# First block of a fused transformer kernel on one core: attention and retention heads in pairs between half tiles of the projections, a first tile by chunks of the input, first loads in row halves

## What is computed

```python
mod = jax.nn.silu(c) @ w_ada[l] + b_ada[l]              # six vectors of 1024: shift, scale, gate, twice
h = rmsnorm(x, g_pre_mix[l]) * (1.0 + scale_m) + shift_m
proj = h @ w_in[l]                                      # 1024 x 3072
rq, rk, rv, rg, aq, ak, av = jnp.split(proj, split_at, axis=-1)
y_ret = bidirectional_retention(...)                    # 4 heads, keys of 64, values of 128, then a norm per head
y_ret = jax.nn.silu(rg) * y_ret
results = [dilated_attention(qh, kh, vh, w, d, slopes) for (w, d) in DILATED_CONFIGS]   # 8 heads of 64
mixed = jnp.concatenate([y_ret, y_att], axis=-1) @ w_out[l]
x = x + gate_m * rmsnorm(mixed, g_post_mix[l])
```

## Time and profile before

| | us |
|---|---|
| median of 3 runs | 2343.58 (2340.36 to 2344.03) |
| the profiled execution, its own time | 2334.57 |
| its span in the trace | 2332.8 |
| TensorE busy in the span | 2016.2 (86%) |
| VectorE, ScalarE busy | 1017.2, 732.0 |
| DMA, mean over the span | 282 GB/s |

### The profile page before, as it was taken

One profiled execution on the slowest core, in us unless ns is written; L12 is line 12 of the kernel. 1 busy time (PEld: TensorE's weight loads), 2 busy tenths in 40 slices (PEclk: granted clock), 3 DMA queues, 4 the chain that ended last, 5 costly groups with the idle time before them and its releaser, 6 DMA issues.

```text
span 2332.8 us, 30652 instructions
## 1 busy us (share of the span) xinstructions
PE 2016.2 (86%) x12663; PEld 1489.7 (64%) x12664; DVE 1017.2 (44%) x1126; ACT 732.0 (31%) x794; POOL 31.7 (1%) x27
## 2 busy tenths in 40 slices
PE   7988867767777677776789999999999999999999
PEld 5858423323232233332278899998888889998887
DVE  5462100000000000000178677777777768777776
ACT  3452101000000000000144446454444444745443
POOL 0000000000000000000000002000000000200000
PEclk8997787888878888877799999999999999999999
DMA  9755699999999999999945565365575566545554
GB/s 327 285 203 242 248 428 428 429 428 428 430 428 428 429 428 428 429 428 428 419 169 179 152 225 181 132 217 181 152 221 187 158 184 208 181 152 192 181 156 133
DMA packets 235194, 657.03 MB, mean 282 GB/s; under 512 B 6932, under 2 KB 121940, under 8 KB 210516
## 3 DMA queue, kind: packets, MB, share of 16 engines
q1 hardware_dynamic: 235092, 655.62, 73.7%
HBM read 654.54 MB, written 1.05 MB: 281 GB/s over the span
## 4 chain that ended last, share of the span: by engine, by line
issue 85%; PE 13%; DVE 1%; POOL 1%; ACT 0%; DVEq 0%; POOLq 0%; ACTq 0%
PE psum L1101 3%; PE psum L1102 2%; PE psum L1123 2%; PE psum L1124 2%; PE psum L1125 2%; PE psum L1202 2%; PE psum L1203 1%; DVE ring_r L1935 1%; PE psum L1169 0%; POOL work L715 0%; ACT ring_r L1466 0%; PE psum L1170 0%; POOL work L714 0%; POOL work L716 0%; DVE x L2231 0%
## 5 line engine op out<-in xcount | busy, mean ns | idle before, releaser
L1935 DVE TENSOR_TENSOR ring_r<-ring,ring_r 128x2048 fp32r<-128x2048 f32 (+2 forms) x182 | 452.6, 2517 | 100.9 <-ACT ring_r L1466 100.1
L1101 PE MATMUL psum<-work_r,ring_r 128*128 128x512 f32 x1280 | 448.6, 396 | 3.5 <-DVE ring_r L1935 3.5
L1466 ACT CAST ring_r<-ring 128x2048 fp32r<-128x2048 f32 (+2 forms) x180 | 360.0, 2040 | 289.0 <-PE psum L1203 120.0
L1102 PE MATMUL psum<-work_r,ring_r 128*128 128x256 f32 x1280 | 358.0, 280 | 0.0
L1101 PEld LDWEIGHTS psum<-work_r,ring_r 128*128 128x128 f32 x1280 | 240.1, 188 | 61.2 <-issue 4.0
L1123 PE MATMUL psum<-work_r,ring_r 128*128 128x256 f32 x928 | 263.5, 284 | 2.5 <-DVE ring_r L1935 2.5
L1124 PE MATMUL psum<-work_r,ring_r 128*128 128x256 f32 x928 | 262.3, 283 | 0.0
L1125 PE MATMUL psum<-work_r,ring_r 128*128 128x256 f32 x928 | 262.0, 282 | 0.0
L1018 PE MATMUL psum<-ring,work 128*32 128x512 f32 x1536 | 216.0, 718 | 42.8 <-DMA ring<-in_w_up_e_dram 41.0
L1202 PE MATMUL psum<-work_r,ring_r 128*128 128x512 f32 x704 | 246.0, 395 | 3.0 <-DVE ring_r L1935 3.0
L1102 PEld LDWEIGHTS psum<-work_r,ring_r 128*128 128x128 f32 x1280 | 241.4, 189 | 0.0
(11 more groups left out here) (295 smaller groups left out, 2439.1 us busy)
## 6 DMA issues: line engine op xcount, KB each, us to landing
ring<-in_w_gate_e_dram SPq DMA_DIRECT2D x64, 2048.0 KB, 12.4
ring<-in_w_down_e_dram SPq DMA_DIRECT2D x48, 2048.0 KB, 31.7
ring<-in_ffn_w_up_dram SPq DMA_DIRECT2D x41, 2048.0 KB, 8.0
ring<-in_w_up_e_dram SPq DMA_DIRECT2D x32, 2048.0 KB, 21.4
work<-in_w_up_e_dram SPq DMA_DIRECT2D x32, 2048.0 KB, 30.1
ring<-in_w_in_dram SPq DMA_DIRECT2D x26, 2048.0 KB, 8.1
ring<-in_ffn_w_down_dram SPq DMA_DIRECT2D x32, 1408.0 KB, 7.1
work<-in_w_down_e_dram SPq DMA_DIRECT2D x16, 2048.0 KB, 37.6
```

What stands on the lines that cost most here:

```text
L1101: pe.matmul(dst, w_hi[:, k, cols], h_both(k), start=(k == 0), stop=False)
L1102: mm = pe.matmul(dst[:, 0:S], w_lo[:, k, cols], h_hi_[:, S * k:S * (k + 1)], start=False, stop=(k == KD - 1))
L1466: act.copy(hi_unit(name, unit), raw_unit(name, unit)).then_inc(hi_ready, 1)
L1935: dve.tensor_tensor(lo_unit(name, unit), raw_unit(name, unit), hi_unit(name, unit).bitcast(F32), ALU.subtract).then_inc(lo_ready, 1)
```

## The change

It rewrites the order of the first block and some of its buffers. (1) The tiles `ada` 0 to 3 are loaded as two pairs, each in two DMAs of four row chunks with 1024 columns in one piece; TensorE takes the four modulations as halves (`half_modulation`) with small matmuls between (`warm`). (2) The attention's tiles come first (`WIN`), the first of them in two DMAs, split chunk by chunk and multiplied chunk by chunk over all four column blocks (`head_tile`). The small loads now go ahead of the second `win` tile. (3) The other tiles are done in half tiles (`win_unit`), with an eviction for each half (`evict`), and the heads stand between them, two heads at a time: scores with the two heads on the upper and the lower 64 rows of the array, without zeroed halves, values on its left and right 64 columns. (4) The retention's values are centred by VectorE when they leave PSUM (`values_centred`), which replaces the mean matmul on the result. (5) `wout` is multiplied in four parts by chunks of the input, those of the attention first, with the retention's norm between them. (6) Slots 6 and 7 are released after the last head, and `EXPERT_SLOTS` begins with them.

The core of the diff (the new order of TensorE in full, of ScalarE and VectorE in parts):

```diff
+WIN = (3, 4, 5, 0, 1, 2)
...
-    order = [("ada", 0), ("ada", 1), ("ada", 2), ("ada", 3), ("win", 0), ("win", 1), ("ada", 4), ("win", 2), ("ada", 5),
-             ("win", 3), ("ada", 6), ("win", 4), ("ada", 7), ("win", 5), ("ada", 8), ("wout", 0), ("wout", 1),
-             ("ada", 9), ("ada", 10), ("ada", 11)]
-EXPERT_SLOTS = (2, 1, 3, 0, 4, 5, 6, 7, 8)
+    order = [("ada", 0), ("ada", 1), ("ada", 2), ("ada", 3), ("win", 3), ("win", 4), ("ada", 4), ("ada", 5), ("win", 5),
+             ("ada", 6), ("win", 0), ("ada", 7), ("win", 1), ("ada", 8), ("win", 2), ("ada", 9), ("wout", 0),
+             ("ada", 10), ("wout", 1), ("ada", 11)]
+EXPERT_SLOTS = (6, 7, 2, 3, 0, 1, 4, 5, 8)
...
+            def pair_half(i, half):
+                first = slot_view(("ada", i), KD, 512)
+                pair = ring[:, i:i + 2, :].rearrange("p s n -> p (s n)").rearrange("p (k n) -> p k n", k=KD)
+                src = a["w_ada"][0].rearrange("(k p) n -> p k n", p=P)
+                ks = slice(4 * half, 4 * half + 4)
+                sp.dma_start(pair[:, ks, :], src[:, ks, 512 * i:512 * i + 1024]).then_inc(loaded[i + half], 16)
+            for i in (0, 2):
+                for half in range(2):
+                    pair_half(i, half)
+            for name, _, _, _ in first_tiles()[4:]:
...
+                if name == ("win", 3):
+                    sp.wait_ge(tile_done[0], 1)
+                    view, src = slot_view(name, KD, 512), columns(w, 512 * i, 512)
+                    sp.dma_start(view[:, 0:4], src[:, 0:4]).then_inc(head_loaded, 16)
+                    sp.dma_start(view[:, 4:8], src[:, 4:8]).then_inc(loaded[0], 16)
...
+            def half_modulation(i, half):
+                pair = ring[:, i // 2 * 2:i // 2 * 2 + 2, :].rearrange("p s n -> p (s n)").rearrange("p (k n) -> p k n", k=KD)
+                w = pair[:, :, 512 * (i % 2):512 * (i % 2) + 512]
+                for k in range(4 * half, 4 * half + 4):
+                    g = k % 4
+                    mm = pe.matmul(mod_bank(i)[32 * g:32 * g + 32, :], silu_c[:, k, :], w[:, k, :],
+                                   start=(half == 0), stop=(half == 1), skip_group_check=True)
+                return mm
...
+            def warm(n):
+                for _ in range(n):
+                    pe.matmul(bank[5][:, 0:P], ident[:], ident[:], start=True, stop=True)
...
+            for i in (0, 2):
+                if i:
+                    pe.wait_ge(mod_ready, 2)
+                pe.wait_ge(loaded[i], 16)
+                half_modulation(i, 0)
+                half_modulation(i + 1, 0).then_inc(tile_done[i], 1)
+                if i:
+                    pe.wait_ge(scaled_ready, 1)
+                    warm(5)
+                pe.wait_ge(loaded[i + 1], 16)
+                half_modulation(i + 1, 1).then_inc(rows_done, 1)
+                half_modulation(i, 1).then_inc(tile_done[i + 1], 1)
+                modulation_columns(i + 1)
                 modulation_columns(i)
...
+            def head_tile():
+                pe.wait_ge(x_ready, 4)
+                name = ("win", 3)
+                for k in range(KD):
+                    h_chunk(k)
+                    pe.wait_ge(head_lo, k + 1)
+                    tokens = slice(S * k, S * (k + 1))
+                    for c in range(4):
+                        w_hi, w_lo = hi_unit(name, c // 2), lo_unit(name, c // 2)
+                        out_c, cols = two_banks[0][:, S * c:S * (c + 1)], slice(P * (c % 2), P * (c % 2 + 1))
+                        pe.matmul(out_c, w_hi[:, k, cols], h_hi_[:, tokens], start=(k == 0 and c % 2 == 0), stop=False,
+                                  skip_group_check=True)
+                        pe.matmul(out_c, w_hi[:, k, cols], h_lo_[:, tokens], start=False, stop=False, skip_group_check=True)
+                        mm = pe.matmul(out_c, w_lo[:, k, cols], h_hi_[:, tokens], start=False, stop=(k == KD - 1),
...
+            def win_unit(n):
+                i, half = WIN[n // 2], n % 2
                 name = ("win", i)
-                if i == 1:
-                    pe.wait_ge(x_ready, 4)
-                if i >= 2:
-                    pe.wait_ge(proj_ready, i - 1)
-                dst = two_banks[i % 2]
...
+            def att_scores(c):
+                if c == 0:
+                    pe.wait_ge(unit_evicted, 4)
+                    pe.wait_ge(ident_r_ready, 1)
+                else:
+                    pe.wait_ge(att_max_ready, 2 * c)
                 for t in range(TT):
-                    mm = pe.matmul(score_bank(hd)[:, S * t:S * (t + 1)], aq[hd % 2][:, c, P * t:P * (t + 1)],
-                                   ak[:, c, :], start=True, stop=True)
+                    for j in range(2):
+                        mm = pe.matmul(bank[4 + j][:, S * t:S * (t + 1)], aq[HALF * j:HALF * (j + 1), c, P * t:P * (t + 1)],
+                                       ak[HALF * j:HALF * (j + 1), c, :], start=True, stop=True)
...
+            def att_values(c):
+                if c == 0:
+                    pe.wait_ge(unit_evicted, 6)
+                pe.wait_ge(att_pT_ready, 2 * c + 2)
                 for s in range(TT):
-                    mm = pe.matmul(two_banks[1][at:at + ATT_DIM, S * c:S * (c + 1)],
-                                   av[:, s, ATT_DIM * hd:ATT_DIM * (hd + 1)], pT_att[:, s, :],
-                                   start=(s == 0), stop=(s == TT - 1), skip_group_check=True)
+                    for j in range(2):
+                        hd = 2 * c + j
+                        mm = pe.matmul(two_banks[1][HALF * j:HALF * (j + 1), S * c:S * (c + 1)],
+                                       av[:, s, ATT_DIM * hd:ATT_DIM * (hd + 1)], pT_att[:, j, s, :],
+                                       start=(s == 0), stop=(s == TT - 1), skip_group_check=True)
                 mm.then_inc(att_done, 1)
...
+            head_tile()
+            modulation(4)
+            layer_columns()
+            win_unit(2)
+            modulation_columns(4)
+            win_unit(3)
+            modulation(5)
+            att_scores(0)
+            win_unit(4)
+            modulation_columns(5)
+            win_unit(5)
+            att_transpose(0)
+            att_scores(1)
+            win_unit(6)
+            modulation(6)
+            att_transpose(1)
+            win_unit(7)
+            att_values(0)
+            att_transpose(2)
+            att_scores(2)
+            modulation_columns(6)
+            win_unit(8)
+            modulation(7)
+            att_transpose(3)
+            win_unit(9)
+            att_values(1)
+            att_transpose(4)
+            att_scores(3)
+            modulation_columns(7)
+            win_unit(10)
+            modulation(8)
+            att_transpose(5)
+            ret_scores(0)
+            win_unit(11)
+            att_values(2)
+            att_transpose(6)
+            modulation_columns(8)
+            ret_values(0)
+            ret_values(1)
+            ret_scores(1)
+            modulation(9)
+            att_transpose(7)
+            modulation_columns(9)
+            ret_values(2)
+            ret_values(3)
+            att_values(3)
+            modulation(10)
+            pe.wait_ge(att_done, ATT_HEADS // 2)
+            pe.wait_ge(ret_done, RET_HEADS)
+            for s in (6, 7):
+                pe.sem_inc(tile_done[s], 1)
+            def group_variances():
...
+            def wout_products(i, blocks, ks, opens=False, closes=False):
+                name = ("wout", i)
+                for c in blocks:
+                    unit, cols = c // 2, slice(P * (c % 2), P * (c % 2 + 1))
+                    pe.wait_ge(first_lo_ready, first_splits.ready(name, unit, 0))
+                    w_hi, w_lo = hi_unit(name, unit), lo_unit(name, unit)
+                    out_c = wout_banks(i)[:, S * c:S * (c + 1)]
+                    for k in ks:
+                        tokens = slice(S * k, S * (k + 1))
+                        pe.matmul(out_c, w_hi[:, k, cols], mixin_hi[:, tokens],
...
+            pe.wait_ge(mixin_lo_ready, 1)
+            wout_products(0, (0, 1), (4, 5), opens=True)
+            group_variances()
+            modulation_columns(10)
+            pe.wait_ge(mixin_lo_ready, 2)
+            wout_products(0, (0, 1), (6, 7))
+            spread_columns(grstd_ready, 1, two_banks[2], RET_HEADS * TT, grstd_spread)
+            wout_products(0, (2, 3), (4, 5, 6, 7), opens=True)
+            pe.wait_ge(centred_ready, 2)
+            wout_products(1, (0, 1), (4, 5, 6, 7), opens=True)
+            modulation(11)
+            wout_products(1, (2, 3), (4, 5, 6, 7), opens=True)
+            modulation_columns(11)
+            pe.wait_ge(mixin_lo_ready, 4)
             for i in range(2):
-                split_products(("wout", i), two_banks[i], mixin_hi, mixin_lo, mixin_chunk if i == 0 else None)
-            for s in range(SPLIT_SLOTS, SLOTS):
+                wout_products(i, (0, 1, 2, 3), (0, 1, 2, 3), closes=True)
+            for s in (4, 5, 8):
...
```

(26 more changed lines are left out.)

587 lines of the change are left out of this document (311 added, 276 removed).

## The result

| | before | after |
|---|---|---|
| median, 19 runs each (us) | 2339.91 (2332.74 to 2351.85) | 2325.22 (2317.03 to 2341.3) |
| the profiled execution, its own time | 2334.57 | 2326.23 |
| its span in the trace | 2332.8 | 2324.4 |

The ratio is 0.9941, with a 95% interval from 0.9924 to 0.9957: 13.8 us less (10.1 to 17.8). 14.5 were forecast.

The account below looks back on a forecast made before the run. TensorE's work and waits up to the end of `wout`, which hold back the expert load stream, were taken as the bound. 36.0 + 135.1 + 18.0 = 189.1 against 203.56: 14.5 us less, 2329 us, range 2318 to 2338.

Parts of the forecast that it names:

- What sets the end: Ahead of the experts: the load stream waits for the first expert, so a microsecond saved before `wout`'s end counts fully.
- The start: Up to the first `win` product: paired half modulations and chunked splitting bring it from 39.42 to 36.0, 3.4 us less.
- Work: TensorE from first product to end of `wout`: 146.2 us falls to 135.1, 11.1 less, from paired heads and no mean matmul.
- Waits: TensorE's waits up to the end of `wout`: 17.8 summed, 18 taken, nearly as before; bounds 8 and 28.
- Columns 5: VectorE copies the modulation's row after the split of `win` 0, so TensorE waits 3.6 us.
- Transposes 2: Exponentials, eviction and sums stand behind the split of `win` 1: a wait of 3.1 us, and 0.8 for head 0.
- Transposes 6: Four decay tables and the split of `wout` 0 stand between: a wait of 3.6 us, and 0.8 ahead of it.
- Modulation behind half tile 3: VectorE adds the last modulation's bias only after the next tile's split: TensorE waits 1.1 us.
- Columns 9: A TensorE wait of 1.4 us ahead of these modulation columns.
- The 3.4 in the first tile: VectorE needs some 1.5 us a chunk for TensorE's 1.44, first ones at half clock: a wait of 3.4 us.
- the upper bound: Waits of 28 us, if gaps of some 3 us also cost half-clock stretches and ScalarE's order one more wait per tile.
- the first rival: Paired halves run one after the other, +5.2, and mode changes, +1.4: gain only 7.9 us, 2336; chance 0.12.

Follow-up runs that it names:

- e4: Changed kernel with ScalarE's and VectorE's ready work moved ahead of splits that wait for a load, TensorE's order untouched: 2310.92 us, 0.9881; again 2311.07, 0.9885.
- e7: Changed kernel with the first tile's loops turned round, all eight input chunks for each block of 128 columns: first tile 20.3 us, end of `wout` 201.66.
- e5: Changed kernel with both attention heads of a pair on the same half of the array, output not the reference's: end of `wout` 189.22 instead of 191.86.
- e1: Changed kernel with paired score and value loops turned round, both matmuls of one head first: pairs 1.07 and 1.02 us, end of `wout` 201.38.
- e8: Changed kernel with the first four tiles loaded one DMA per 512-column tile instead of row halves of pairs: first product 39.39, end of `wout` 199.96.
- e6: Changed kernel with slots 6 and 7 released at the end of `wout` and experts beginning with slots 2, 3, 0, 1: expert to layers 938.8 us.
- e3: Changed kernel with the four retention decay tables made earlier instead of ahead of the softmax of heads 6 and 7: end of `wout` 191.75.
- e10: Reordered ScalarE and VectorE version of the changed kernel (e4), plus both heads of a pair on one half of the array: 2318.10 us, 0.9893.

## Why the prediction was right, step by step

- **What sets the end.** Right. 11.7 us at the end of `wout` were 11.2 where the stream waits and 11.6 at the layers. The start of the layers can still lose some 4 us to the clock behind the stream, as in e4's first run.
- **The start.** 36.0 forecast. With the same order on TensorE and the second pair at full clock 37.28, 36.26, 36.0 (three times), 35.8 and 34.5 were read; with that pair at half clock 39.1, 39.1 and 39.4, and 37.9 in e7. In the changed kernel's profile the norm's small matmuls (L758) ended 1.5 us later than before. The steps are right, but the clock's play of nearly 5 us is larger than the 3.4 us forecast, and the forecast didn't have it.
- **Work.** Value pairs 1.0 as taken. Score pairs 1.06 for the 0.86 taken: six times 0.2 is 1.2 us too little. The 0.2 may hold the change of mode that the Trainium skill's page TensorEngine Tiling (Array Packing), section Key Properties, has drain the engine; no run here separates it. Row groups overlap, as the Trainium skill's page TensorE: Matmul & The Clock Gate, Part 3, has it, and the trace agrees: 1.06 against 1.92. The spread was priced at 3.1 from a row whose granted clock was 0.62; at full clock in e4 it takes 150.36 - 148.66 = 1.7, which happens to cancel the scores. TensorE's work behind the first tile was 135.1 - 11.55 = 123.6 by my sum and 125.4 at full clock in e4. Most of that difference is in the half tiles: one runs from 123.35 to 129.29 there, 5.94 us for the 5.78 of half of 11.55.
- **Waits.** 18 forecast, 17.5 found, but not the same ones. Columns 5: 3.6, found 2.29. Transposes 2: 3.1, found 2.04, and 0.8 for head 0, found none. Transposes 6: 3.6 and 0.8 ahead, found 3.53 and 0.73. Modulation behind half tile 3: 1.1, found 2.00. Columns 9: 1.4, found 0.23. The 3.4 in the first tile did not come (0.1), since no part of it ran at half clock. So the idle time is 10.8, and in place of the rest stand 6.7 us at a lower clock, mostly behind waits, which I had only in the upper bound. That the sum came out at 18 is luck.
- **The part that failed: the sum's form.** I added TensorE's work and its waits as if each stood for itself, and so charged the first rival, halves one after the other with changes of mode, 6.6 us more than the forecast, which would have left it a gain of 7.9. e5 put the attention's halves one after the other, 6.9 us of work, and cost nothing. Where a wait ends at a time that ScalarE and VectorE set, work in front of it is free, and so are savings. In the changed kernel a saving on attention pairs of 6.9 us is worth nothing; it is worth 9.8 in e4. So the 11.7 us can't be credited to the pairing. By stages they are 2.1 at the first product, 2.8 in the first tile (14.5 us before, its end at 53.91, against 11.7) and 6.8 behind it (149.7 against 142.9). Two stages of before, with the columns of the earlier trace rows:

```profile
39.42:53.91 14.49, 14.16 (x96) 13.48 (x97) 11.70 (x17) 7.77 (x7) 0.00 (x0) 0.87 0.92 296
53.91:203.56 149.65, 138.77 (x937) 111.41 (x935) 72.52 (x141) 61.11 (x81) 0.00 (x0) 0.98 0.59 211
```

The 2.8 us are thus nearly all clock (0.87, behind a wait of 4.21, against 1.00), with 0.3 of short waits. In e1, e4 and e8, where the clock was low in the changed order too, the tile ended at 53.4 to 53.8, hardly earlier than 53.91: how much of the 4.9 us up to there the change brings in a usual run is open, with one profile of before. Behind the tile TensorE idles as long before as after, 10.9 and 10.8 us, and its busy time fell. How the 6.8 split over the order, the half tiles, the pairs and the centring wasn't tried.
- **Costless parts.** Longer rows: no wait for them either way, e8. Small loads ahead of the second tile: no wait of TensorE at that tile. Early release: nothing at the start. The layers' tiles: I called the slot order harmless for them, and it is as the change has it; e6 shows a neighbour of it that costs 6.

## What to carry to other kernels

A saving on the engine that seems to be the bound counts only as far as no wait behind it ends at a time set by the others; before pricing it, look whether the next wait's releaser depends on that engine. In queues with a fixed order, put everything that is ready ahead of an instruction that waits for a load: here this took out 17 us with no work removed, more than the 13.8 of the change itself. When slots are reassigned, follow the list to the end of the loop, to the tile that is loaded last and the one that takes its slot.

## What the runs showed of the chip

- A few microseconds of waiting can cost more than themselves. Behind the 3.53 us wait ahead of transposes 6 the granted clock fell (0.58 from 142.5 to 150, which holds the end of the wait), and so it did in every profile that had this wait. Behind 2.0 to 2.8 us waits it fell in some profiles (0.77 in both stretches of e3) and stayed at 1.00 in others (90 to 120 in the changed kernel). The length of the wait alone doesn't decide: in e5 it stayed at 1.00 from 65.55 to 90, behind a wait of 3.39.
- The clock also fell with TensorE busy without a gap, once after a run of matmuls that use half the array. e10 from 113.8 us on, behind a value pair, transposes and a score pair, 4.4 us together (columns: PE, PEclk, DMA share, GB/s):

```profile
114.00:117.00 3.00, 3.00 (x15) 1.00 1.00 304
117.00:120.00 3.00, 3.00 (x19) 0.91 1.04 397
120.00:123.00 3.00, 3.00 (x17) 0.52 0.35 128
```

In e4, where the same three take 2.7 us, it stayed at 1.00. But it also stayed at 1.00 in e10 itself, from 90 to 102, around the same three at 94.94. So e10's 9.8 us are 6.9 us of work and 3 us of clock; whether the halves bring the clock down was not tested.
